# One core, one kernel: sums over later keys by a reversed scan on VectorE instead of matmuls, and three small broadcasts by transposing

## The reference, cut to what matters

```python
z  = q @ k.T / 8                      # where key < query, else -inf
sp = softplus(z)
between[q, s] = sum of sp[q, j] over keys j > s
w  = exp(z - sp - between);  out = w @ v
```

```python
y_diag = ((C @ B.T) * exp(a_cs[l] - a_cs[s]) for s <= l) @ x
```

## Time and profile before

| what | value |
|---|---|
| median of three runs | 1353.65 us (1351.85 to 1354.17) |
| the profiled execution | 1353.55 us, of which the span of the instructions 1351.5 us |
| TensorE matmuls busy | 1341.1 us, 99% of the span, 6878 records |
| TensorE weight loads busy | 1110.9 us, 82% |
| VectorE, ScalarE, GpSimd busy | 619.2, 513.2 and 597.9 us: 46%, 38%, 44% |
| granted TensorE clock, mean | 0.997 |

### The profile page before, as it was taken

One profiled execution on the slowest core, in us unless ns is written; L12 is line 12 of the kernel. 1 busy time (PEld: TensorE's weight loads), 2 busy tenths in 40 slices (PEclk: granted clock), 3 DMA queues, 4 the chain that ended last, 5 costly groups with the idle time before them and its releaser, 6 DMA issues.

```text
span 1351.5 us, 17866 instructions
## 1 busy us (share of the span) xinstructions
PE 1341.1 (99%) x6878; PEld 1110.9 (82%) x6878; DVE 619.2 (46%) x1050; ACT 513.2 (38%) x751; POOL 597.9 (44%) x448
## 2 busy tenths in 40 slices
PE   9999999999999999999999999999999999999998
PEld 8888887788888888888888887877898888888887
DVE  3665434466544533313321347777765232242233
ACT  6222444555532453212211226345555223433233
POOL 4452333325445544545544446443332643526441
PEclk9999999999999999999999999999999999999999
DMA  6331242412232543233323323322312322322321
GB/s 204 94 96 61 79 119 68 140 47 79 79 109 64 163 112 99 94 94 93 93 94 99 103 78 107 104 66 68 98 64 63 121 80 79 101 87 94 96 91 63
DMA packets 146177, 126.43 MB, mean 94 GB/s; under 512 B 4352, under 2 KB 143744, under 8 KB 146112
## 3 DMA queue, kind: packets, MB, share of 16 engines
q1 hardware_dynamic: 145904, 125.40, 30.3%
q10 hardware_dynamic: 208, 0.12, 0.0%
HBM read 120.66 MB, written 2.10 MB: 91 GB/s over the span
## 4 chain that ended last, share of the span: by engine, by line
PE 96%; DVE 2%; ACT 1%; issue 0%; DMA 0%; SPq 0%; ACTq 0%; DVEq 0%
PE gemm L570 25%; PE gemm L571 25%; PE gemm L578 25%; PE gemm L623 2%; PE gemm L624 2%; PE gemm L627 2%; PE gemm L593 2%; PE gemm L597 2%; PE gemm L594 2%; PE mix L961 1%; PE mix L949 1%; PE mix L1017 1%; PE mix L776 1%; PE mix L649 0%; PE mix L800 0%; PE mix L759 0%
## 5 line engine op out<-in xcount | busy, mean ns | idle before, releaser
L505 POOL TENSOR_TENSOR wlo<-raw,whi 128x512 fp32r<-128x512 f32 x424 | 572.6, 1381 | 564.6 <-ACT whi L1113 564.6
L570 PE MATMUL gemm<-hh,whi 128*128 128x512 f32 x1128 | 445.0, 394 | 0.5 <-ACT whi L1113 0.4
L571 PE MATMUL gemm<-hl,whi 128*128 128x512 f32 x1128 | 440.4, 390 | 0.0
L578 PE MATMUL gemm<-hh,wlo 128*128 128x512 f32 x1128 | 280.2, 390 | 0.0
L1113 ACT ACTIVATE whi<-raw 128x2048 fp32r<-128x2048 f32 x106 | 202.4, 1910 | 192.7 <-PE gemm L578 166.1
L570 PEld LDWEIGHTS gemm<-hh,whi 128*128 128x128 f32 x1128 | 212.4, 188 | 49.0 <-issue 4.3
L571 PEld LDWEIGHTS gemm<-hl,whi 128*128 128x128 f32 x1128 | 212.4, 188 | 43.2 <-issue 0.2
L578 PEld LDWEIGHTS gemm<-hh,wlo 128*128 128x128 f32 x1128 | 211.3, 188 | 43.7
L501 POOL TENSOR_TENSOR wlo_b<-raw_b,whi_b 128x512 fp32r<-128x512 f32 x16 | 20.6, 1291 | 152.2 <-ACT whi L1113 152.2
L1842 DVE TENSOR_TENSOR fu_t<-gemm,R 128x512 f32<-128x512 f32 x22 | 15.2, 692 | 99.7 <-PE gemm L578 99.7
L570 PE MATMUL gemm<-ah,whi 128*128 128x512 f32 x132 | 51.4, 390 | 0.5 <-DVE xT L1821 0.5
(11 more groups left out here) (463 smaller groups left out, 1981.8 us busy)
## 6 DMA issues: line engine op xcount, KB each, us to landing
raw<-w_in SPq DMA_DIRECT2D x55, 1024.0 KB, 5.3
raw<-w_gu SPq DMA_DIRECT2D x44, 512.0 KB, 4.8
raw<-w_o SPq DMA_DIRECT2D x8, 1024.0 KB, 4.9
raw<-w_down SPq DMA_DIRECT2D x16, 512.0 KB, 4.3
raw_b<-w_branch SPq DMA_DIRECT2D x16, 256.0 KB, 5.6
raw<-w_ao SPq DMA_DIRECT2D x4, 1024.0 KB, 4.9
raw<-w_so SPq DMA_DIRECT2D x4, 1024.0 KB, 5.0
raw<-w_down SPq DMA_DIRECT2D x8, 384.0 KB, 3.4
```

What stands on the lines that cost most here:

```text
L505: last = nc.gpsimd.tensor_tensor(a(wlo), a(raw), as_f32(a(whi)), ALU.subtract)
L570: mm(bank[:, :], w, xh[:, k, :], start=(k == 0), stop=False)
L571: mm(bank[:, :], w, xl[:, k, :], start=False, stop=False)
L578: last = mm(bank[:, :], wlo_[:, s, k, col:col + P], xh[:, k, :], start=False, stop=(k == kts - 1))
```

## The change

- `st1`: z is now computed with queries on partitions, by the same kinds of matmuls as in `mo1`. VectorE first adds a mask to the four diagonal blocks in PSUM; ScalarE then takes abs, exp and ln as before. VectorE writes max(z, 0) into `stsp`, and four `tensor_tensor_scan` instructions over reversed rows (512, 384, 256 and 128 columns) add it and the ln part up from the last key to the first. VectorE subtracts that from z, and ScalarE takes the last exp: all of it before any engine but TensorE leaves `st1`.
- `st2`: TensorE transposes the ten blocks of the weights, ScalarE copies them from PSUM to `stp`. The 20 matmuls with `tri`, the parts `st_h` and `st_l`, and the masks L1721 and L1737 are gone.
- `mh1`: TensorE transposes the column of `acs`, broadcast over 128 columns, four times. `spread`, `adtb`, `adtb_l`, `upper_r` are gone.
- The factor 1/rms: four such transposes of `rcol` instead of the diagonal matrices.
- `acs`: four matmuls instead of ten, with the later sums batched.
- `cb`: two of the four matmuls take copies `bmx`, `cmx` on the other 64 partitions. SyncE issues the four DMAs that swap them after the load of unit 7, and waits there for `ya` and `silu`.
- The constants shrink from 1024 to 640 columns, and three roundings of constants on ScalarE are gone.

```diff
@@ -374,6 +369,12 @@
                 if n >= 1:
                     slot_free(n)
                     load(n, cols(w_in, c, UC))
+                if n == 7:
+                    sp.wait_ge(sem("ya"), 2)
+                    sp.wait_ge(sem("silu"), 4)
+                    for half, whole in ((bmx, bm), (cmx, cm)):
+                        for to in (0, 64):
+                            sp.dma_start(half[to:to + 64, :], whole[64 - to:P - to, :]).then_inc(sem("bc_swapped"), 16)
                 if n == 1:
                     sp.dma_start(c1[:, P:], cst1[:, P:]).then_inc(sem("c1_in"), 16)
...
@@ -696,11 +697,12 @@
 
             def st_acs():
                 pe.wait_ge(sem("adt"), 1)
-                for n in range(TT):
-                    o = M[3][:, n * HEADS:(n + 1) * HEADS]
-                    for m in range(n + 1):
-                        last = mm(o, u_incl if m == n else ones, adt[:, m * HEADS:(m + 1) * HEADS],
-                                  start=(m == 0), stop=(m == n))
+                mm(M[3][:, 0:TT * HEADS], u_incl, adt, start=True, stop=False)
+                for m in range(TT - 1):
+                    later = TT - 1 - m
+                    last = mm(M[3][:, (m + 1) * HEADS:TT * HEADS], ones,
+                              adt[:, m * HEADS:(m + 1) * HEADS].unsqueeze(1).broadcast_to((P, later, HEADS)),
+                              start=False, stop=(m == TT - 2))
                 last.then_inc(sem("acs_ps"), 1)
 
             def st_cb(g):
@@ -710,23 +712,21 @@
                     pe.wait_ge(sem("xdt"), 2)
                 else:
                     pe.wait_ge(sem("y_mid"), 1)
-                gs = slice(64 * g, 64 * g + 64)
-                for n, (_, w) in enumerate(REG):
+                pe.wait_ge(sem("bc_swapped"), 64)
+                own, other = head_rows(g), head_rows(g + 1)
+                for n, (r, kk, qq) in ((0, (own, bm, cm)), (1, (other, bmx, cmx)), (2, (own, bm, cm)), (3, (other, bmx, cmx))):
                     b, c = RBANK[n]
-                    last = mm(M[b][:, c:c + w], bm[gs, n * P:(n + 1) * P], cm[gs, n * P:SEQ], start=True, stop=True)
+                    last = mm(M[b][:, c:c + REG[n][1]], kk[r, n * P:(n + 1) * P], qq[r, n * P:SEQ], start=True, stop=True)
                 last.then_inc(sem("cb_ps"), 1)
 
             def st_mh1(h):
-                pe.wait_ge(sem("adtb"), h + 1)
                 if h == 0:
                     pe.wait_ge(sem("acs"), 1)
-                    pe.wait_ge(sem("rounded_consts"), 3)
                 else:
                     pe.wait_ge(sem("seg"), h)
-                for m in range(TT):
-                    for part in (adtb, adtb_l):
-                        last = mm(M[3][:, m * P:SEQ], part[:, m, :], upper_r[:, 0:SEQ - m * P],
-                                  start=(m == 0 and part is adtb), stop=(m == TT - 1 and part is adtb_l))
+                for t in range(TT):
+                    sums = acs[:, t * HEADS + h:t * HEADS + h + 1].broadcast_to((P, P))
+                    last = nc.tensor.transpose(M[3][:, t * P:(t + 1) * P], sums, ident)
                 last.then_inc(sem("acsb_ps"), 1)
 
             def st_mh2(h):
@@ -792,35 +792,29 @@
                     pe.wait_ge(sem("tile_free"), tiles_before(12))
                     pe.wait_ge(sem("yd_lo"), HEADS)
                 else:
-                    pe.wait_ge(sem("st_arg"), h)
+                    pe.wait_ge(sem("st_pt"), 3 * h)
                 pe.wait_ge(sem("swapped"), 128)
                 x, y = array_halves(h, qb, kb)
-                for n, (q, k) in ((0, x), (1, y), (3, y), (2, x)):
-                    b, o = RBANK[n]
-                    last = mm(M[b][:, o:o + REG[n][1]], k[:, n * P:(n + 1) * P], q[:, n * P:SEQ], start=True, stop=True)
+                for c, (q, k) in ((3, x), (2, y), (0, y), (1, x)):
+                    b, o = QBANK[c]
+                    w = (c + 1) * P
+                    last = mm(M[b][:, o:o + w], q[:, c * P:(c + 1) * P], k[:, 0:w], start=True, stop=True)
                 last.then_inc(sem("st_z"), 1)
 
             def st_st2(h):
-                pe.wait_ge(sem("rounded_consts"), 2)
-                pe.wait_ge(sem("st_lo"), h + 1)
+                pe.wait_ge(sem("st_w"), h + 1)
                 for n in (0, 1, 3, 2):
                     b, o = RBANK[n]
-                    a, w = REG[n]
-                    for part in (st_h, st_l):
-                        last = mm(M[b][:, o:o + w], tri[:, 0:P], part[:, a:a + w], start=(part is st_h),
-                                  stop=(n == TT - 1 and part is st_l))
-                    for m in range(n + 1, TT):
-                        a, w = REG[m]
-                        for part in (st_h, st_l):
-                            last = mm(M[b][:, o + (m - n) * P:o + REG[n][1]], tri[:, P:], part[:, a:a + w],
-                                      start=False, stop=(m == TT - 1 and part is st_l))
-                last.then_inc(sem("st_b"), 1)
+                    for c in range(n, TT):
+                        a = QREG[c][0] + n * P
+                        last = nc.tensor.transpose(M[b][:, o + (c - n) * P:o + (c - n + 1) * P], stl[:, a:a + P], ident)
+                last.then_inc(sem("st_t"), 1)
 
             def st_st3(h):
-                pe.wait_ge(sem("st_w"), h + 1)
+                pe.wait_ge(sem("st_pt"), 3 * h + 3)
                 if h >= 1:
                     pe.wait_ge(sem("yb_lo"), h)
-                attend(M[3], vb, stl, h, "st_o")
+                attend(M[3], vb, stp, h, "st_o")
 
             stages = {"dt": st_dt, "dtT": st_dtT, "xsT": st_xsT, "acs": st_acs, "cb": st_cb, "mh1": st_mh1, "mh2": st_mh2,
                       "mn": st_mn, "mo1": st_mo1, "mo2": st_mo2, "mo3": st_mo3, "st1": st_st1, "st2": st_st2,
...
@@ -833,9 +827,9 @@
 
                         pe.wait_ge(sem("c1_in"), 16)
                         pe.wait_ge(sem("x_kept"), KD - 4)
-                        pe.wait_ge(sem("rdiag"), 1)
+                        pe.wait_ge(sem("rcol"), 1)
                         for t in range(TT):
-                            last = mm(M[0][:, t * P:(t + 1) * P], ones, xbuf[:, t, 0:P], start=True, stop=True)
+                            last = nc.tensor.transpose(M[0][:, t * P:(t + 1) * P], rcol[:, t:t + 1].broadcast_to((P, P)), ident)
                         last.then_inc(sem("r_ps"), 1)
                     run_mix(stages, 2 * n + j)
                 if n in (8, 11):
...
@@ -1213,26 +1204,31 @@
 
             def st_st1(h):
                 act.preload_act_table_set(EXP_LN)
-                act.wait_ge(sem("st_z"), h + 1)
+                act.wait_ge(sem("st_m"), h + 1)
                 if h >= 1:
-                    act.wait_ge(sem("st_o"), h)
-                for i, (b, c, a, w) in enumerate(RUNS):
-                    last = fn(stl[:, a:a + w], M[b][:, c:c + w], ACT.Abs)
+                    act.wait_ge(sem("st_t"), h)
+                for c in range(TT):
+                    b, o = QBANK[c]
+                    a, w = QREG[c]
+                    last = fn(stl[:, a:a + w], M[b][:, o:o + w], ACT.Abs)
                 last.then_inc(sem("st_abs"), 1)
                 act.wait_ge(sem("st_abs"), h + 1)
                 fn(stl[:, :], stl[:, :], ACT.Exp, scale=-1.0).then_inc(sem("st_exp"), 1)
                 act.wait_ge(sem("st_exp"), h + 1)
                 fn(stl[:, :], stl[:, :], ACT.Ln, bias=1.0).then_inc(sem("st_ln"), 1)
                 act.preload_act_table_set(EXP_TANH)
-
-                act.wait_ge(sem("st_sp"), h + 1)
+                act.wait_ge(sem("st_arg"), h + 1)
+                fn(stl[:, :], stl[:, :], ACT.Exp).then_inc(sem("st_w"), 1)
+
+            def st_st2(h):
+                act.wait_ge(sem("st_t"), h + 1)
                 if h >= 1:
-                    act.wait_ge(sem("st_b"), h)
-                fn(st_h[:, :], stsp[:, :], ACT.Copy).then_inc(sem("st_hi"), 1)
-
-            def st_st2(h):
-                act.wait_ge(sem("st_arg"), h + 1)
-                fn(stl[:, :], stl[:, :], ACT.Exp).then_inc(sem("st_we"), 1)
+                    act.wait_ge(sem("st_o"), h)
+                for b, c, a, w in (RUNS[0], RUNS[2]):
+                    fn(stp[:, a:a + w], M[b][:, c:c + w], ACT.Copy).then_inc(sem("st_pt"), 1)
+                for b, c, a, w in (RUNS[1], RUNS[3]):
+                    last = fn(stp[:, a:a + w], M[b][:, c:c + w], ACT.Copy)
+                last.then_inc(sem("st_pt"), 1)
 
             def st_st3(h):
                 out_hi(M[3], "st_o", yh[0], "yb_hi", h)
...
             tt(fgng, pcol("fg", 0, 8), pcol("ng2", 0, 8), ALU.mult)
 
-            dve.wait_ge(sem("rcol"), 1)
-            for t in range(TT):
-                last = ts(xbuf[:, t, 0:P], ident, rcol[:, t:t + 1], None, ALU.mult)
...
 
-            def spread(h):
-                dve.wait_ge(sem("adt"), 1)
-                if h >= 1:
-                    dve.wait_ge(sem("acsb_ps"), h)
-                a = adt.rearrange("p (t h) -> p t h", h=HEADS)[:, :, h:h + 1]
```

(95 more changed lines are left out.)

## The result

The changed kernel takes 1339.17 us (median of four runs, 1338.61 to 1340.38), the kernel before on the same chip 1352.75 us. The ratio is 0.9901, with a 95% interval of 0.9888 to 0.9914. The forecast was 1339.3 us. The profiled execution took 1338.61 us, its span is 1336.6 us.

A forecast was written before the change was run, and what follows sets the result against it. TensorE's queue, running without gaps, was taken to bound the kernel. Savings of 6.64 + 2.49 + 0.45 + 1.34 + 1.60 + 1.72 = 14.24 us off 1353.55 gave 1339.3 us, range 1336.8 to 1344.5.

The forecast's parts named there:

- The wait of L776: Slot 20, TensorE waiting for VectorE's product: 0.44 us now, 1.25 us after, so head 2's 0.83 us is lost.
- the nine waits of before: TensorE's waits in the kernel before: nine rows, 5.1 us in all, so its queue runs without gaps.
- The repeated column: Rival in `mh1` and 1/rms: a repeated column is turned at half speed, 0.45 us more in four places, 1341.1; chance 0.05.
- The clock: Behind `acs`, 100 to 110 us: clock no longer falls, 1.6 us saved; rival that a fall is left, chance 0.16.
- The cover of `st1`: Longer `st1` on ScalarE and VectorE stays hidden: 3.3 us left ahead of `lo_done`, against 1.5 or 3.5 us needed.
- S: Time of the scans in `st1`: taken as 1.7 us, 3.7 kept for the range; 2.7 by the skill's rule.
- a late `st1`: Rival: at 5 us of scans, heads 1 and 3 stand for `lo_done` 1.5 us each, 1342.3; chance 0.09.
- Transposes and the clock: Rival: the four long turning stages each let the clock fall, 6.4 us in all, 1345.7; chance 0.03.
- SyncE's queue: Four DMAs ahead of unit 8's load delay it by 2.1 us, to 84.2; hidden, since its rounding waits for TensorE.

The follow-up runs named there:

- e4: The kernel before with only the stick-breaking part of the change (`st1` to `st3`): 1346.76 us against 1353.45.
- e5: The kernel before with only `mh1` by transposes of a repeated column, without `spread`: 1350.96 us against 1353.45.
- e6: The changed kernel with `mh1` of head 2 ahead of `cb` of group 1 in slot 19, copy and mask of `cb` moved too: 1337.77 us.
- e9: The kernel before with ScalarE's rounding of `upper_r` moved behind the rounding of unit 4's weights: 1352.81 us against 1351.66.

## Why the prediction was right, point by point

- *`st2`*: 4 x 1.66 forecast, 4 x 1.66 measured, in the change and alone (e4).
- *`mh1`*: 0.83 for three heads and nothing for head 2 forecast. Slots 15 to 18 gave 2.59 for one `cb` and two `mh1` (0.86 + 1.66 = 2.52), slots 19 to 21 gave 1.74 for one of each (1.69). e5 shows the loss of head 2 by itself, e6 takes it back. The wait of L776 was forecast at 1.25 us and is 1.1. The forecast also had 5.1 us for the nine waits of before together; the rows add up to 4.7, which changes nothing. The repeated column is turned at the speed of any other block (0.44): that rival is out.
- *1/rms, `acs`, `cb`*: 0.45, 1.34 and 0.86 each, as measured.
- *The clock*: 1.60 us were counted in full, with bounds of 0 and 1.6. Against the profiled execution this came true (`acs` and the clock together: 2.94 forecast, 2.91 measured), but not as a property of the kernel: before had the fall in about half of its executions. Of the four executions of before that the result is measured against, two are in the lower group (1351.77 and 1351.85 us). Against these the gain is 12.6, and the sum without this term was 12.64. Against the median of before it is 13.58, 0.66 less than the 14.24 forecast. The forecast time of 1339.3 us fits to 0.1 because 14.24 was taken off an execution with the fall, 1353.55 us. That this one was profiled is chance.
- *Missed*: 0.29 us. The text of the change was weighed for what ScalarE does more, not for what it does less: the rounding of `upper_r` stood ahead of weights for which TensorE waited (e9). A further 0.24 us are gained up to 21 us. The same eight matmuls start between 20.98 and 21.81 us in the other profiled executions, in no order of their kernels, so this is put down to chance; no run shows its cause.
- *The cover of `st1`*: forecast to hold, and it did. S, the time of the four scans, was taken as 1.7 and is 2.97; the bounds held it. 0.5 us of cover is left for `lo_done` by the trace; the forecast would have had 0.5 at that S (3.3 - 2.8). In the upper end of the range, 1344.5, the 1.8 us for a late `st1` follow from no S in the text (3.7 gives 0.4, 5 gives 3.0); nothing hangs on it here.
- *Transposes and the clock*: the rival did not come: the clock is 1.00 in every stretch of ten microseconds from 60 to 370 us, and the four new stages of ten transposes, 1.09 us each, lie in it. The Trainium skill ("TensorE: Matmul & The Clock Gate", section "Part 4: PE-mode transpose") says that transposes do not count as busy for the full clock. That rule did not bear on this case; no run here has a longer stretch of them.
- *SyncE's queue*: the four swaps were issued from 80.41 to 82.91, the next load at 82.95, where 84.2 was forecast. Hidden, as said.

## What to carry to other kernels

Where one engine's queue is full from end to end, price an edit by its stretch in the chain that ended last, and then ask at each consumer whether the work that stood between a producer and it is still there: the one loss in this change was a tile that had become too short for a chain of other engines, and turning two neighbours round took it back. Count what an edit takes from the helper engines too, where it stood ahead of something that is waited for. Before a fall of the clock goes into a sum, look at several executions: a profile shows one of them.

## What the runs showed of the hardware

- A `tensor_tensor_scan` over a row read and written backwards takes 2.0 ns for an element of float32, about 1.9 times a plain subtraction with one operand in PSUM (687 ns for 512 and 278 ns for 128 in L1733 of before), plus about 165 ns.
- 20 records of matmuls four columns wide (2.13 us) are followed by nine matmuls in 3.64 us, at 1.2 GHz for the most part, in the profiled execution of before; by the times, about half of its executions (27 of 56) have such a fall. With 40 records the profiled execution has the fall inside the stretch, and the times of all five call for one; with 8 records none of eleven does.
- A transpose of one column repeated 128 times costs the same 0.11 us as one of a full 128x128 float32 block.
